# Two chunks in one matmul for the last two levels of a delta-rule inverse

## What is computed

```python
lower = jnp.where(strict, jnp.einsum("bhncd,bhnsd->bhncs", k_beta, k) * decay, 0.0)
t_inv = lax.linalg.triangular_solve(eye + lower, jnp.broadcast_to(eye, lower.shape),
                                    left_side=True, lower=True, unit_diagonal=True)
u = jnp.einsum("bhncs,bhnse->bhnce", t_inv, v_beta)
w = jnp.einsum("bhncs,bhnsd->bhncd", t_inv, k_beta * eg[..., None])
```

## Time and profile before

| what | us |
| --- | --- |
| median of three runs | 2164.04 |
| lowest and highest | 2163.17, 2166.78 |
| span of the profiled execution, first to last instruction | 2162.6 |
| PE busy | 2111.2 (98%) |
| DVE busy | 1328.5 (61%) |
| ACT busy | 858.6 (40%) |
| POOL busy | 417.3 (19%) |

### The profile page before, as it was taken

One profiled execution on the slowest core, in us unless ns is written; L12 is line 12 of the kernel. 1 busy time (PEld: TensorE's weight loads), 2 busy tenths in 40 slices (PEclk: granted clock), 3 DMA queues, 4 the chain that ended last, 5 costly groups with the idle time before them and its releaser, 6 DMA issues.

```text
span 2162.6 us, 29667 instructions
## 1 busy us (share of the span) xinstructions
PE 2111.2 (98%) x10266; PEld 1728.8 (80%) x10266; DVE 1328.5 (61%) x1917; ACT 858.6 (40%) x1352; POOL 417.3 (19%) x325
## 2 busy tenths in 40 slices
PE   6999999999999899999999999999999999999998
PEld 4788888888888788888888888888777778888886
DVE  6877888777554444443567555533888866555431
ACT  3333333333232232222235545422666645444321
POOL 0455775555600400000110000011000000000021
PEclk8999999999999999999999999999999999999999
DMA  7344443344333323333332333333122132333332
GB/s 288 105 120 126 116 113 110 106 114 119 108 97 115 109 85 95 95 95 96 95 102 81 95 97 97 92 97 102 49 59 59 44 93 84 96 95 95 96 93 73
DMA packets 394816, 216.82 MB, mean 100 GB/s; under 512 B 7880, under 2 KB 391298, under 8 KB 393219
## 3 DMA queue, kind: packets, MB, share of 16 engines
q1 hardware_dynamic: 393939, 213.51, 33.6%
q0 software_dynamic: 288, 2.10, 0.3%
q10 hardware_dynamic: 528, 0.40, 0.1%
HBM read 211.79 MB, written 4.19 MB: 100 GB/s over the span
## 4 chain that ended last, share of the span: by engine, by line
PE 83%; DVE 10%; ACT 3%; issue 2%; DMA 1%; SPq 1%; POOL 0%; DVEq 0%; POOLq 0%; ACTq 0%
PE ps L2227 25%; PE ps L2229 24%; PE ps L2228 24%; PE ps L2403 4%; DVE w_lo L1318 1%; PE ps L2254 1%; DMA ada<-w_ada 1%; DVE gd_v_s L1474 1%; DVE small L2109 1%; DVE a_sb L2142 1%; DVE a_t_lo L2118 1%; ACT at_swap L1209 1%; ACT prob L1232 0%; DVE prob L2137 0%; PE ps L2732 0%
## 5 line engine op out<-in xcount | busy, mean ns | idle before, releaser
L2227 PE MATMUL ps<-h_hi,w_hi 128*128 128x512 f32 x1896 | 769.5, 406 | 7.7 <-DVE h_lo L1382 5.5
L2229 PE MATMUL ps<-h_hi,w_lo 128*128 128x512 f32 x1896 | 742.8, 392 | 0.0
L2228 PE MATMUL ps<-h_lo,w_hi 128*128 128x512 f32 x1896 | 741.0, 391 | 0.0
L1318 DVE TENSOR_TENSOR w_lo<-raw,w_hi 128x1024 fp32r<-128x1024 f32 x334 | 435.0, 1303 | 351.3 <-ACT w_hi L815 350.6
L815 ACT ACTIVATE w_hi<-raw 128x1024 fp32r<-128x1024 f32 x336 | 355.6, 1059 | 635.8 <-PE ps L2229 570.0
L2227 PEld LDWEIGHTS ps<-h_hi,w_hi 128*128 128x128 f32 x1896 | 357.7, 189 | 83.2 <-issue 17.0
L2229 PEld LDWEIGHTS ps<-h_hi,w_lo 128*128 128x128 f32 x1896 | 357.0, 188 | 77.4
L2228 PEld LDWEIGHTS ps<-h_lo,w_hi 128*128 128x128 f32 x1896 | 358.4, 189 | 64.3
L2227 PE MATMUL ps<-act_hi,w_hi 128*128 128x512 f32 x528 | 206.2, 390 | 0.0
L2229 PE MATMUL ps<-act_hi,w_lo 128*128 128x512 f32 x528 | 205.7, 390 | 0.0
L2228 PE MATMUL ps<-act_lo,w_hi 128*128 128x512 f32 x528 | 205.6, 389 | 0.0
(11 more groups left out here) (385 smaller groups left out, 2585.0 us busy)
## 6 DMA issues: line engine op xcount, KB each, us to landing
raw<-ffn_w_up SPq DMA_DIRECT2D x88, 512.0 KB, 3.7
raw<-w_in SPq DMA_DIRECT2D x72, 512.0 KB, 3.7
raw<-w_ffn_in SPq DMA_DIRECT2D x44, 512.0 KB, 3.7
ada_w<-w_ada SPq DMA_DIRECT2D x32, 512.0 KB, 3.8
raw<-ffn_w_down SPq DMA_DIRECT2D x32, 512.0 KB, 3.8
raw<-diff_w_qkv SPq DMA_DIRECT2D x24, 512.0 KB, 3.7
ada<-w_ada SPq DMA_DIRECT2D x8, 1024.0 KB, 12.5
ada_w<-w_ada_f SPq DMA_DIRECT2D x16, 512.0 KB, 3.7
```

The source lines that it names most:

```text
L1318: nc.vector.tensor_tensor(w_lo[:, tile.slot], raw[:, tile.raw], w_hi[:, tile.slot].bitcast(F32), SUB)\
L2227: nc.tensor.matmul(dst, w_hi[:, tile.slot, k], hi, start=first, stop=False)
L2228: nc.tensor.matmul(dst, w_hi[:, tile.slot, k], lo, start=False, stop=False)
L2229: return nc.tensor.matmul(dst, w_lo[:, tile.slot, k], hi, start=False, stop=last)
```

## The change

The products of levels 4 and 5 are made for two chunks at a time. The stationary operand is 128 columns, 64 of each of two chunks; the moving operand holds the columns of both chunks; the result is twice as high and twice as wide, and of it only the quarters in which both sides come from the same chunk are read (half the result). Chunk j of a pair has its result in partitions 64 j to 64 j + 63. So the readers (DVE's copies and transposes, ACT's copies) are split in two by j. For level 5 the stationary half of `low` must lie next to that of the other chunk: POOL packs it into `low_h` (a part of the tile `dia`), a new step "low_half" behind modulation 2, for which y5 on PE and, at the end, `short_in` on DVE now wait.

```diff
-POOL_STEPS = ["k_norm"] + [f"mask{_n}" for _n in range(WHOLE_LEVELS)] + ["low_pairs", "ada", "o_norm"]
+POOL_STEPS = ["k_norm"] + [f"mask{_n}" for _n in range(WHOLE_LEVELS)] + ["low_pairs", "low_half", "ada", "o_norm"]
...
-        y_half, u_half = [ps[0:64, b, 0:2 * P].rearrange("p (n c) -> p n c", n=NC) for b in (4, 6)]
-        x_half = ps[0:64, 5, 0:P].rearrange("p (n c) -> p n c", n=NC)
+        def two_by_two(v):
+
+            return v.rearrange("p (a j c) -> p a j c", a=2, j=2)
+
+        y_two, u_two = [two_by_two(ps[:, b, 0:2 * P]) for b in (4, 6)]
+        x_two = two_by_two(ps[:, 5, 0:P])
...
-                for j in (2, 3, 4, 5):
+                modulation(2)
+
+                pool.wait_ge(g_pe, step(PE_STEPS, f"y{WHOLE_LEVELS - 1}", h))
+                nc.gpsimd.tensor_tensor(low_h.rearrange("p (n c) -> p n c", n=NC), chunks(gd["low"][:])[:, :, 64:P],
+                                        ones[:, 0:64].unsqueeze(1).to_broadcast([P, NC, 64]), MULT).then_inc(g_pool, 1)
+                for j in (3, 4, 5):
                     modulation(j)
...
-                        nc.scalar.activation(in_quadrant(gd["x_t"][:], 1)[:, :, 0:32], x_half[quadrant(0)], ACT.Copy)\
-                          .then_inc(g_act, 1)
+                        for j in range(2):
+                            x_new = nc.scalar.activation(in_quadrant(gd["x_t"][:], 1)[:, j::2, 0:32], x_two[quadrant(2 * j), :, j], ACT.Copy)
+                        x_new.then_inc(g_act, 1)
...
-                        for pair in range(2):
-                            y = nc.vector.tensor_copy(gd["y_t"][quadrant(2 * pair + 1), 0:P].rearrange("p (n c) -> p n c", n=NC),
-                                                      y_half[quadrant(pair), :, quadrant(pair)])
+                        for j in range(2):
+                            for pair in range(2):
+                                y = nc.vector.tensor_copy(two_by_two(gd["y_t"][quadrant(2 * pair + 1), 0:P])[:, :, j],
+                                                          y_two[quadrant(2 * j + pair), :, j, quadrant(pair)])
...
-                        nc.vector.tensor_copy(gd["y_t"][64:P, 0:2 * P], bank(4)[0:64, 0:2 * P]).then_inc(g_dve, 1)
+                        for j in range(2):
+                            y = nc.vector.tensor_copy(two_by_two(gd["y_t"][64:P, 0:2 * P])[:, :, j], y_two[64 * j:64 * j + 64, :, j])
+                        y.then_inc(g_dve, 1)
...
-                    for n in range(NC):
-                        ins = nc.tensor.matmul(y_half[:, n], low_s[:, 64 * n:64 * n + 64], halves(x_t[:], 0)[:, n], start=True, stop=True)
+                    for a in range(2):
+                        ins = nc.tensor.matmul(y_two[:, a], low_s[:, P * a:P * a + P], halves(x_t[:], 0)[:, 2 * a:2 * a + 2], start=True, stop=True)
...
-                    for n in range(NC):
-                        ins = nc.tensor.matmul(x_half[:, n], u_s[:, 64 * n:64 * n + 64], y_t[:, 32 * n:32 * n + 32], start=True, stop=True)
+                    for a in range(2):
+                        ins = nc.tensor.matmul(x_two[:, a], u_s[:, P * a:P * a + P], y_t[:, 64 * a:64 * a + 64], start=True, stop=True)
...
-                        ins = nc.tensor.matmul(y_half[:, n], part(gd["low"], n)[:, 64:P], part(x_t, n)[:, 0:64], start=True, stop=True)
+                        ins = nc.tensor.matmul(y_two[:, a], low_h[:, P * a:P * a + P], two(x_t[:], a)[:, :, 0:64], start=True, stop=True)
...
+                    else:
+                        pe.wait_ge(g_pool, step(POOL_STEPS, "low_half", h))
```

More of the change, by code:

```diff
@@ L354, in block_kernel @@
         low_part = (gd["low_d"], gd["dia"])
-        low_s, u_s = gd["low_d"][:, 0:2 * P], gd["low_d"][:, 2 * P:4 * P]
+        low_s, u_s, low_h = gd["low_d"][:, 0:2 * P], gd["low_d"][:, 2 * P:4 * P], gd["dia"][:, 0:2 * P]
         ada_w = sb("ada_w", [P, 2, KD, P], at=work + 2048 * len(names))
@@ L1033, in head @@
                         after_pe(f"x{n}")
-                        nc.scalar.activation(in_quadrant(gd["x_t"][:], 1)[:, :, 0:32], x_half[quadrant(0)], ACT.Copy)\
-                          .then_inc(g_act, 1)
+                        for j in range(2):
+                            x_new = nc.scalar.activation(in_quadrant(gd["x_t"][:], 1)[:, j::2, 0:32], x_two[quadrant(2 * j), :, j], ACT.Copy)
+                        x_new.then_inc(g_act, 1)
                     else:
                         after_pe(f"u{n}")
-                        nc.scalar.activation(chunks(gd["u_t"][:])[0:64, :, 64:P], u_half[:], ACT.Copy).then_inc(g_act, 1)
+                        for j in range(2):
+                            u_new = nc.scalar.activation(chunks(gd["u_t"][:])[0:64, j::2, 64:P], u_two[64 * j:64 * j + 64, :, j], ACT.Copy)
+                        u_new.then_inc(g_act, 1)
                     if more and n in (0, 2, 4):
@@ L1553, in short_in @@
                     if more:
-                        dve.wait_ge(g_pool, step(POOL_STEPS, "low_pairs", h))
+                        dve.wait_ge(g_pool, step(POOL_STEPS, "low_half", h))
                         dve.wait_ge(g_pe, step(PE_STEPS, f"y{LEVELS - 1}", h))
@@ L1686, in head @@
                         after_act(f"x{n}")
-                        for pair in (1, 0):
-                            u = nc.vector.transpose(in_quadrant(gd["u_t"][:], 2 * pair)[:, :, quadrant(2 * pair + 1)],
-                                                    x_half[quadrant(pair)])
+                        for j in range(2):
+                            for pair in range(2):
+                                u = nc.vector.transpose(in_quadrant(gd["u_t"][:], 2 * pair)[:, j::2, quadrant(2 * pair + 1)],
+                                                        x_two[quadrant(2 * j + pair), :, j])
                         u.then_inc(g_dve, 1)
@@ L2404, in by_chunk, with two @@
                     return ins
+                def two(v, a):
+                    return chunks(v)[:, 2 * a:2 * a + 2]
                 def lower_pairs():
-                    for n in range(NC):
-                        ins = nc.tensor.matmul(y_half[:, n], low_s[:, 64 * n:64 * n + 64], halves(x_t[:], 0)[:, n], start=True, stop=True)
+                    for a in range(2):
+                        ins = nc.tensor.matmul(y_two[:, a], low_s[:, P * a:P * a + P], halves(x_t[:], 0)[:, 2 * a:2 * a + 2], start=True, stop=True)
                     return ins
                 def inverse_pairs():
-                    for n in range(NC):
-                        ins = nc.tensor.matmul(x_half[:, n], u_s[:, 64 * n:64 * n + 64], y_t[:, 32 * n:32 * n + 32], start=True, stop=True)
+                    for a in range(2):
+                        ins = nc.tensor.matmul(x_two[:, a], u_s[:, P * a:P * a + P], y_t[:, 64 * a:64 * a + 64], start=True, stop=True)
                     return ins
                 def lower_half():
-                    for n in range(NC):
-                        ins = nc.tensor.matmul(y_half[:, n], part(gd["low"], n)[:, 64:P], part(x_t, n)[:, 0:64], start=True, stop=True)
+                    for a in range(2):
+                        ins = nc.tensor.matmul(y_two[:, a], low_h[:, P * a:P * a + P], two(x_t[:], a)[:, :, 0:64], start=True, stop=True)
                     return ins
                 def inverse_half():
-                    for n in range(NC):
-                        ins = nc.tensor.matmul(u_half[:, n], y_t[:, 64 * n:64 * n + 64], part(u_t, n)[:, 64:P], start=True, stop=True)
+                    for a in range(2):
+                        ins = nc.tensor.matmul(u_two[:, a], y_t[:, P * a:P * a + P], two(u_t[:], a)[:, :, 64:P], start=True, stop=True)
                     return ins
```

## The result

The changed kernel takes 2170.6 us in the median of seven runs (2169.06 to 2172.88), the kernel before, which also ran seven times, 2164.0. The ratio is 1.0029, with a 95% interval of 1.0020 to 1.0039: slower by 6.3 us (4.3 to 8.4). The span of the profiled execution is 2167.0 us, 4.4 above that of before. In that execution the first y4 product starts at 107.91 us, 1.87 earlier than before, after a stretch that the change does not touch, and this makes its span look better than the median.

What follows compares the result with a forecast made beforehand. DVE, with POOL's shift, was taken to bound seven HEAD passes and PE the last head: 7 x 0.91 - 1.5 = +4.9 us, giving 2168.9 us; range 2164.5 to 2172.5, the forecast's own 2167.5 to 2170.5.

Steps and rivals of the forecast that it cites:

- The bound in HEAD: In the seven HEAD passes, from the tap in front of y4 to w, DVE is the chain, PE's matmuls beside it.
- PE's saving of 0.37 us a product: On PE, each new product takes 0.45 us instead of 0.82; four products save 1.48 us a head.
- POOL's packing: Between modulations 2 and 3 in HEAD, low_half delays POOL's multiply, so DVE's w_lo behind it ends 0.76 us later.
- The y4 copies: On DVE in HEAD, four copies take 0.92 us instead of 0.61; the +0.31 hides in w_lo's wait for POOL.
- The transposes: On DVE in HEAD, x4's transposes go from two to four, 0.57 to about 0.91 us; the +0.34 just fits its cover.
- The cover of 0.38: In HEAD, L1482's wait for POOL's first add, within which up to 0.38 us more of transposes cost nothing.
- y5 copies: On DVE in HEAD, two copies of 0.29 us replace one of 0.42: +0.15 us a pass.
- LAST: In the eighth head, y4 to w falls from 10.05 to 8.6 us, since no wait is shown there.
- I count the whole: In LAST, PE's saving on four products counts in full: -1.5 us.
- the port taken in the other order: Rival: in HEAD, w_lo comes before POOL's multiply; +0.32 us a pass, +0.7 in all, 2164.8 us; chance 0.15.
- PE-bound: Rival: PE sets the pace, so all eight heads save 1.48 us: -11.8, 2152.2 us; chance 0.08.
- Costs do not hide: Rival: whole-price small operations and late PE handovers make a HEAD pass cost 1.3 to 1.4 us: +8, 2172; chance 0.15.

Runs made afterwards that it cites:

- the first kernel with y on ACT: Changed kernel with low's packing moved from POOL to ACT and DVE's y4 and y5 copies made by ACT: 2161.9 us, ratio 0.9984 to the kernel before.
- the last kernel: Changed kernel with packing and y4, y5 copies on ACT, and DVE's w_lo moved behind the taps in HEAD: 2157.7 us, ratio 0.9963 to the kernel before.

## Why the prediction was right, and where it was not

- **The bound in HEAD** was read rightly: DVE, not PE, ends the way from y4 to w. PE's saving of 0.37 us a product was seen (L2429 stands in 0.44 us, estimated 0.45, where the old product took 0.82: in LAST the fill in front starts at 571.84 and the second fill behind at 572.74, less 0.46), and in HEAD it became waiting. The form with 64 moving columns, which no row had shown, stands in 0.45 as well (LAST of the first kernel with y on ACT, 564.70 to 565.61, less 0.46).
- **POOL's packing**: +0.76 was forecast, +0.79 stands in the changed kernel, +0.77 in the kernel with nothing else. That it acts through the turn-taking of the two engines is shown by w_lo in the kernel with the packing alone, which is 2.88 long instead of 2.10 and ends 1.09 behind POOL's multiply; with the packing on ACT the pass falls back by 0.78.
- **The y4 copies**: 0.96 instead of 0.92, hidden behind L1330, as forecast.
- **The transposes** were mis-sized: 1.05 us from the first to what follows, where I had scaled 0.91. The cover of 0.38 was there (L1494 takes 0.69 now), but they overran it: +0.48 - 0.39. That and the **y5 copies** (+0.17, forecast +0.15) bring the pass to 1.07 instead of 0.91: 7 x 0.16 = 1.1 us of the miss. What I had missed stands in the earlier trace rows: L1482 is issued at 437.04, 0.06 before the transposes end, and I scaled the 0.57 with that overlap in it. In the changed kernel the operation behind does not overlap them, nor do the two y5 copies overlap each other.
- **LAST** was the larger error in kind. I forecast 8.6 us from y4 to w because no wait was shown there; it is 9.63. The step that failed is "I count the whole": I followed POOL's shift in a HEAD pass and not in LAST. LAST before:

```profile
564.98 2.97 POOL L729 TENSOR_TENSOR ada_w<-ada_w 128x512 f32<-128x512 f32 x2
566.13 1.22 DVE L1318 TENSOR_TENSOR w_lo<-raw,w_hi 128x1024 fp32r<-128x1024 f32 x1
```

  The row of POOL holds two adds, the first 1.29 long, so L1318 was issued 0.14 us before that add ended (566.27), 1.15 behind its start, and lost nothing. POOL's packing shifts this by 0.74: L1330 is issued 0.41 behind the start of the same add. In the changed kernel:

```profile
571.37 1.28 POOL L733 TENSOR_TENSOR ada_w<-ada_w 128x512 f32<-128x512 f32 x1
571.78 1.95 DVE L1330 TENSOR_TENSOR w_lo<-raw,w_hi 128x1024 fp32r<-128x1024 f32 x1
573.76 0.93 DVE L1659 COPY gd_y_t<-ps 32x64 f32<-32x64 f32 x4
...
574.74 0.66 PE L2435 MATMUL ps<-gd_y_t,gd_low_d 128*128 128x64 f32 x4 [0.70 <-DVE gd_y_t L1659]
```

  L1330 ends 1.08 us behind the add (572.65), 1.95 long where it was 1.22, and x4 waits 0.70. From y4 to x4 it is 2.67 us, where the same products without a wait take 1.82 (563.11 to 564.93 in LAST of the first kernel with y on ACT), and 0.11 more is lost behind it. That is 0.96 of the 1.03 missing.
- **The sum**: the terms of the trace are now 7 x 1.07 - 0.4 - 0.1 (y4 itself is reached 0.1 earlier) = +7.0. The runs show +6.3, 4.3 to 8.4; forecast +4.9. Both errors went the same way and none hid the other. The median of 2170.6 lies just above the 2167.5 to 2170.5 that I gave the forecast itself, and inside the wider range that takes in the rivals.
- **The rivals**: the port taken in the other order did not occur, L1330 waits in every pass. PE-bound, the rival of the other side, is refuted for this kernel. Of its 11.8 us the last kernel has 8.0, where both DVE's copies and its w_lo were moved away, and 5 of them come from the products. "Costs do not hide" (1.3 to 1.4 a pass) did not occur either: the pass costs 1.07.

## What to carry to other kernels

A cheaper operation on the busiest engine is worth nothing where another engine hands it its operands late; follow the operand's way through the pass before counting the saving, and count what the new layout does to that other engine. An operation put on an idle engine is not free when that engine and the one on the chain exclude each other at SBUF: look for what runs directly behind it, and do so again in every stage in which the two engines stand differently in time. Here the change paid only after the copies and the w_lo were out of the way.

## What the runs showed of the hardware

- A 32x64 transpose out of PSUM took 0.236 to 0.254 us, where one of 32x128 took about 0.31: half the elements, four fifths of the time. Four together took 1.05 us to the start of what follows in the changed kernel and 0.94 in the kernel with split copies alone, by whether the operation behind overlapped the last of them (by 0.06) or not. Two 64x128 copies that both read partitions 0 to 63 of PSUM started 0.21 apart; two that read 0 to 63 and 64 to 127 started 0.30 apart. Four 32x64 copies took 0.91 and 0.92 in the two kernels.
- DVE with two SBUF inputs and POOL's element-wise operations took turns by whole operations in every case looked at, and the waiting one ended at its own length less a start of about 0.14 us behind the other (1.08 for 1.22). DVE operations that read PSUM kept their time beside POOL (taps 2.53 and 2.54). By the Trainium skill (SBUF — State Buffer, Who interferes with whom) a DVE instruction with at most one SBUF input, outside the 2-port modes, does not contend with GpSimd. The taps have one tensor input in PSUM and one in SBUF, and agree.
- Where PE had waited for its operands, the product took 0.11 us more: 0.66 instead of 0.55 at x4 and 0.71 instead of 0.60 at u5. Behind a wait its first weight load starts together with the first matmul (438.19 at x4 in the changed kernel), where without one it stands 0.18 ahead (427.71 for 427.89 in the last kernel of the table).
